# A five-deep weight ring with the rest written over the landed unit, and an earlier gather for the first expert, in a one-core decoder layer

## The chip, the cores and the metric

The kernel runs on one core of one Trainium2 chip. The metric is the device time of one execution in microseconds (us). The core has five engines that run their own instruction streams and meet at semaphores: TensorE (PE in the rows, its weight loads PEld), VectorE (DVE), ScalarE (ACT), GpSimd (POOL) and SyncE (SP, which here only issues DMAs). MB is 10^6 bytes.

## The reference

One layer of a decoder on 256 tokens of width 2048, all in float32:

```
h = RMSNorm(x);  p = h @ W_in          # latent q and kv of MLA, rope key, stick-breaking q, k, v
x = x + concat(RMSNorm(o_MLA), RMSNorm(o_SB)) @ W_out      # 8 heads each, causal
x = x + MemCrossAttn(RMSNorm(x), RMSNorm(mem))             # 4 heads into 256 memory tokens
x = x + HierMoE(RMSNorm(x))            # 4 groups x 8 experts: top-1 group, then top-2 in it
y = RMSNorm(x)                         # an expert: (silu(t @ w_gate) * (t @ w_up)) @ w_down
```

Each of the 32 experts has 4.19 MB in each of w_gate, w_up and w_down: 12.6 MB an expert, 403 MB in all. They are read whatever the routing.

## The kernel before

**The first part, the projections.** A projection is a chunk of 512 columns (chunk KV_LAT has 320), and a chunk is cut into units of two 128-row tiles of the weight: 138 units, numbered in the order of `UNITS`. A unit passes through three rings of `RING` = 4 slots: SP loads it into `w_raw` (line 399), ACT rounds it into `w_hi` (`rounded`, line 1084), DVE writes the rest `w_raw - w_hi` into `w_lo` (`split_w`, line 1452), and PE multiplies hi by hi, hi by lo and lo by hi (lines 546 to 548, and 751 to 753 for one token tile alone). SP loads unit u once unit u-4 is split (semaphore `w_split`); ACT rounds unit u once unit u-4 is used by PE (`w_used`). ACT and DVE run their other work in program order: `rounded(upto)` and `split_w(upto)` stand between the other steps and name the unit up to which the engine goes on before it does the next step. Nearly all of these calls ask for `RING` units more than PE has done at that point.

**What lies between the units.** After the query latent, DVE turns the rotary part of the queries (`rope`, lines 1504 to 1509) at step (Q_PE, 1) of the loop over `LATENT`. The attention runs in a loop of nine steps over 8 heads; PE multiplies two units of the memory projections in each head, and units 90 and 91 of the output projection (W_OUT, 0) and (W_OUT, 1) in the last one. The units of MEM_O are 130 to 137; PE takes 130 to 133 first for token tile 0 and then for token tile 1, and only the second counts as used.

**Transfers ahead.** SP's queue is in order. 16 pieces of 0.5 MB of expert 0 are issued after weight units 102 to 130. After the last weight unit it issues the other half of expert 0's gate and up (`load_first`, 2 x 2.1 MB), then expert 1's gate and up into `gu[1]`, which lies over the weight rings: 1 MB when the memory attention has its values, 2.1 MB when all units are split, 2.1 MB when all but two are used, 3.1 MB at the last. Then expert 2 goes into the buffers of expert 0, in pieces that wait for `first_used` (line 459), which PE counts as expert 0's first k tiles are multiplied.

**Routing and expert 0.** From the router's logits DVE finds the group and the two experts of each token (`max`, `max_index`, `picks`, `sel`), PE ranks the tokens of each expert by multiplying a triangular matrix with `sel` (lines 906 and 907), DVE makes the one-hot matrix `hot_0` of expert 0's tokens (line 1886), PE gathers them (930), ACT copies (1377), PE turns (938), DVE applies the gain (`xe`, 1917), and PE starts expert 0 (953). `keep_running` issues matmuls whose result nobody reads. The expert loop then takes one expert after the other with two weight buffers.

Of the kernel before, what the change touches and what calls it, by code (L numbers as in the profile page):

```python
# [45 lines left out]
RING = 4  # L46
# [68 lines left out]
def layer(nc, x, mem, positions, norm_mix, w_in, norm_q_lat, w_q_b, norm_kv_lat, w_kv_b,  # L115
# [11 lines left out]
    with ctx:  # L127
# [27 lines left out]
        v_mem = place("v_mem", [P, TT, UN])  # L155
        ident = place("ident", [P, P])
# [71 lines left out]
        o_mem = place("o_mem", [P, TT, UN], offset=w_at + 48 * 1024)  # L228
        memo_lo = place("memo_lo", [P, MEM_HEADS, SEQ], F32R, offset=w_at + 52 * 1024)
# [14 lines left out]
        x_slots_0 = place("x_slots_0", [P, UN], offset=sb_mask_at)  # L244
# [104 lines left out]
        def _(sp):  # L349
# [33 lines left out]
            for u, (c, i) in enumerate(UNITS):  # L383
# [6 lines left out]
                if u >= RING:  # L390
                    sp.wait_ge(S("w_split"), u - RING + 1)
# [41 lines left out]
            def load_quarter(b, m, q):  # L433

                w = (w_gate, w_up)[m][0, 1].rearrange("(p k) f -> p (k f)", k=KD)
                k0 = b * KD // 2 + 4 * q
                sp.dma_start(gu[1][:, b, m, 4 * q:4 * q + 4, :].rearrange("p k f -> p (k f)"),
                             w[:, k0 * FE:(k0 + 4) * FE]).then_inc(S(f"gu_loaded1{b}"), 16)
# [12 lines left out]
            load_quarter(1, 0, 0)  # L451
            load_quarter(1, 1, 0)
# [47 lines left out]
        def _(pe):  # L500
# [394 lines left out]
            for t in range(TT):  # L895
# [4 lines left out]
            keep_running(1, 12)  # L900


            pe.wait_ge(S("chosen"), 1)
            sel = rt[:, 528:528 + TT * EXPERTS]
            pe.wait_ge(*chunk_out(CHUNKS - 1))
            pe.matmul(ps[2][:, 0:TT * EXPERTS], before, sel, start=True, stop=False)
            pe.matmul(ps[2][:, EXPERTS:TT * EXPERTS], ones[:, :], sel[:, 0:EXPERTS], start=False,
                      stop=True).then_inc(S("ranked"), 1)
            pe.matmul(ps[3][:, 0:EXPERTS], ones[:, :], sel[:, 0:EXPERTS], start=True, stop=False)
            pe.matmul(ps[3][:, 0:EXPERTS], ones[:, :], sel[:, EXPERTS:TT * EXPERTS], start=False,  # L910
                      stop=True).then_inc(S("counted"), 1)


            def gather(n, first=False):

                if first:
                    pe.wait_ge(S("last_copied"), TT)
                else:
                    pe.wait_ge(S("hot_ready"), n + 1)
                    pe.wait_ge(S("xe_ready"), n)  # L920
                for t in range(TT):
                    if first:
                        pe.wait_ge(S("hot_0_ready"), t + 1)
                    for g in range(NJ):
                        if first:
                            h, rows = hot_0[:, t, :], x_res[:, t, g * UN:(g + 1) * UN]
                        else:
                            h, rows = hot[:, t, :], h_nat[:, t, 4 * g:4 * g + 4, :].rearrange(
                                "p k d -> p (k d)")
                        mm = pe.matmul(ps[4][g * SLOTS:(g + 1) * SLOTS, :], h, rows,  # L930
                                       start=(t == 0), stop=(t == TT - 1))
                mm.then_inc(S("gathered"), 1)

            def gather_turn(n, slots=x_slots):

                pe.wait_ge(S("slots_copied"), n + 1)
                for j in range(NJ):
                    mm = pe.transpose(ps[4][:, j * P:(j + 1) * P], slots[:, j * P:(j + 1) * P],  # L938
                                      ident[:, :])
                mm.then_inc(S("slots_turned"), 1)  # L940

            def gate_up(b, side, loads, first=False):
# [4 lines left out]
                else:  # L947
                    more = 16 + 16 * b
# [114 lines left out]
            expert(0, 0, 1)  # L1063
# [7 lines left out]
        def _(sc):  # L1071
# [95 lines left out]
            rounded(DONE[Q_LAT] + RING)  # L1167
# [31 lines left out]
            for n, (c, i) in enumerate(LATENT):  # L1199
                rounded(POS[(c, i)] + RING)  # L1200
# [28 lines left out]
            for i in range(HEADS + 1):  # L1229
                if i < HEADS:  # L1230
                    rounded(START[MEM_K] + 2 * i + RING)
# [9 lines left out]
                if i == HEADS:  # L1241
                    rounded(START[MEM_K] + 2 * i + RING)
# [30 lines left out]
            rounded(POS[(W_OUT, 1)] + RING)  # L1273
            head_norm(HEADS - 2)
            rounded(POS[(W_OUT, 2)] + RING)
            head_norm(HEADS - 1)
            rounded(POS[(W_OUT + 1, 0)] + RING)
# [8 lines left out]
            for c in range(W_OUT, MEM_Q):  # L1286
                rounded(DONE[c] + RING)
                if c > W_OUT and (c - W_OUT) % 2 == 0:
                    memx_heads((c - W_OUT) // 2 - 1)
            rounded(START[MEM_Q] + 3 + RING)  # L1290
# [49 lines left out]
            for q in range(1, 4):  # L1340
                rounded(DONE[MEM_O + q - 1] + RING)
# [24 lines left out]
            scaled(0)  # L1366
            sc.wait_ge(S("logits_ready"), 1)
# [4 lines left out]
            def slots_copy(n, first=False):  # L1372
                sc.wait_ge(S("gathered"), n + 1)
                if not first:
# [785 lines left out]
```

## Time and profile before

| | |
|---|---|
| median of 3 runs | 1401.48 us (1400.82 to 1402.10) |
| profiled execution, its own time | 1399.43 us |
| its span, first to last instruction | 1397.4 us |
| time around the span | 2.0 us |
| PE busy, share of the span | 1063.6 us, 76% |
| DVE, ACT busy | 535.0 us, 336.2 us |
| mean granted TensorE clock | 0.906 of full |
| bytes moved | 481.71 MB, mean 345 GB/s |

All times in the rows are from the start of the span of that one execution. A released wait is told in brackets: how long the engine was idle before the instruction, and what ended it.

### The profile page before, as it was taken

The numbers are of one execution on the slowest core, as the hardware profiler recorded it, in microseconds if no ns is written. First come the engines' busy times: TensorE is split into PE (matmuls) and PEld (weight loads), VectorE is DVE, ScalarE is ACT, GpSimd is POOL, SyncE is SP. The second block draws the span as 40 slices with busy tenths as digits, with TensorE's granted clock in tenths as the row PEclk, the third lists the DMA queues.
The fourth block names the chain that finished last, engine by engine and source line by source line (L and its number), as shares of the span: only waits on it lengthen the run. The fifth ranks groups of instructions, "written<-read, shape, count | busy, mean of one in ns | idle before, by whom it ended". The sixth has DMA issues, their size and how long they took to land.

```text
span 1397.4 us, 21679 instructions
## 1 busy us (share of the span) xinstructions
PE 1063.6 (76%) x8760; PEld 637.4 (46%) x8760; DVE 535.0 (38%) x1110; ACT 336.2 (24%) x607; POOL 33.5 (2%) x96
## 2 busy tenths in 40 slices
PE   8999999999999987575665667665666656666555
PEld 7888887878888632232322223222222222222222
DVE  5545576566665543222222222222222222223223
ACT  5654456665455401000000000000000000000002
POOL 1000000110001000000000000000000000000001
PEclk9999999999999999888888788888888887889878
DMA  7866653326875899999999999999999999999996
GB/s 239 276 195 181 179 167 109 94 85 234 274 290 187 336 424 427 426 425 425 425 430 426 425 425 426 429 426 426 426 425 426 428 426 426 426 426 428 425 426 288
DMA packets 92468, 481.71 MB, mean 345 GB/s; under 512 B 11590, under 2 KB 21964, under 8 KB 59916
## 3 DMA queue, kind: packets, MB, share of 16 engines
q1 hardware_dynamic: 91932, 478.75, 85.9%
q10 hardware_dynamic: 304, 2.11, 0.4%
q0 software_dynamic: 192, 0.31, 0.1%
q8 instruction: 26, 0.43, 0.1%
q14 instruction: 14, 0.11, 0.0%
HBM read 479.04 MB, written 2.10 MB: 344 GB/s over the span
## 4 chain that ended last, share of the span: by engine, by line
DMA 44%; PE 40%; SPq 6%; ACT 4%; DVE 3%; issue 2%; POOL 0%; ACTq 0%; POOLq 0%; DVEq 0%
DMA gu<-in_w_up 42%; PE ps L546 7%; PE ps L548 7%; PE ps L547 7%; PE ps L953 5%; SPq L413 5%; PE ps L1011 4%; PE ps L930 2%; DMA down<-in_w_down 1%; DVE w_lo L1452 1%; SPq L423 1%; PE ps L513 1%; PE ps L938 1%; PE ps L751 1%; PE ps L753 1%
## 5 line engine op out<-in xcount | busy, mean ns | idle before, releaser
L953 PE MATMUL ps<-gu,xe 128*32 128x256 f32 x4096 | 316.1, 477 | 237.9 <-DMA gu<-in_w_up 237.8
L953 PEld LDWEIGHTS ps<-gu,xe 128*32 128x32 f32 x4096 | 153.2, 136 | 422.4 <-DMA gu<-in_w_up 285.0
L1926 DVE TENSOR_TENSOR x_res<-ps,x_res 128x512 f32<-128x512 f32 x248 | 154.0, 683 | 413.1 <-PE ps L965 413.1
L1452 DVE TENSOR_TENSOR w_lo<-w_raw,w_hi 128x1024 fp32r<-128x1024 f32 (+1 forms) x138 | 164.3, 1200 | 129.9 <-ACT w_hi L1084 127.1
L546 PE MATMUL ps<-w_hi,a_hi 128*128 128x512 f32 (+1 forms) x472 | 185.0, 392 | 0.3 <-DVE w_lo L1452 0.3
L547 PE MATMUL ps<-w_lo,a_hi 128*128 128x512 f32 (+1 forms) x472 | 181.4, 384 | 0.0
L548 PE MATMUL ps<-w_hi,a_lo 128*128 128x512 f32 (+1 forms) x464 | 178.4, 385 | 0.0
L1084 ACT ACTIVATE w_hi<-w_raw 128x1024 fp32r<-128x1024 f32 (+1 forms) x138 | 142.1, 1039 | 130.3 <-PE ps L548 116.5
L1384 ACT ACTIVATE sg<-ps 128x128 f32<-128x128 f32 x31 | 8.6, 278 | 607.9 <-PE ps L953 607.9
L1011 PE MATMUL ps<-down,turned 128*32 128x512 f32 x1024 | 117.2, 595 | 28.6 <-ACT turned L1390 24.4
L546 PEld LDWEIGHTS ps<-w_hi,a_hi 128*128 128x128 f32 x472 | 88.7, 188 | 19.3 <-issue 3.2
L547 PEld LDWEIGHTS ps<-w_lo,a_hi 128*128 128x128 f32 x472 | 88.9, 188 | 16.1
L548 PEld LDWEIGHTS ps<-w_hi,a_lo 128*128 128x128 f32 x464 | 87.2, 188 | 17.4
L965 PE MATMUL ps<-y_sb,turned 32*128 32x512 f32 x496 | 71.7, 647 | 23.5 <-ACT y_sb L1393 23.5
L1011 PEld LDWEIGHTS ps<-down,turned 128*32 128x32 f32 x1024 | 30.6, 109 | 94.2 <-issue 80.1
L1956 DVE TENSOR_TENSOR act<-sg,ps 128x128 f32<-128x128 f32 x31 | 8.9, 287 | 151.7 <-ACT sg L1384 151.7
L930 PE MATMUL ps<-h_nat,hot 128*32 128x512 f32 x496 | 58.9, 592 | 0.0
L1917 DVE TENSOR_TENSOR xe<-ps,g_ffn 128x128 f32<-128x128 f32 x124 | 27.4, 283 | 76.2 <-PE ps L938 76.2
L965 PEld LDWEIGHTS ps<-y_sb,turned 32*128 32x128 f32 x496 | 20.0, 184 | 63.9 <-issue 38.0
L1393 ACT ACTIVATE y_sb<-ps 128x512 f32<-128x512 f32 x31 | 18.5, 597 | 123.6 <-PE ps L1011 123.6
L938 PE MATMUL ps<-ident,x_slots 128*128 128x128 f32 x128 | 21.0, 286 | 22.3 <-ACT x_slots L1377 22.3
L938 PEld LDWEIGHTS ps<-ident,x_slots 128*128 128x128 f32 x128 | 13.4, 141 | 50.4 <-ACT x_slots L1377 50.4
(305 smaller groups left out, 840.5 us busy)
## 6 DMA issues: line engine op xcount, KB each, us to landing
down<-in_w_down SPq DMA_DIRECT2D x124, 1024.0 KB, 23.6
gu<-in_w_gate SPq DMA_DIRECT2D x61, 2048.0 KB, 31.6
gu<-in_w_up SPq DMA_DIRECT2D x60, 2048.0 KB, 36.0
w_raw<-in_w_in SPq DMA_DIRECT2D x56, 512.0 KB, 3.8
w_raw<-in_w_out SPq DMA_DIRECT2D x32, 512.0 KB, 4.8
w_raw<-in_w_mem_kv SPq DMA_DIRECT2D x16, 512.0 KB, 3.8
gu<-in_w_up SPq DMA_DIRECT2D x5, 1024.0 KB, 10.4
down<-in_w_down SPq DMA_DIRECT2D x8, 512.0 KB, 5.6
```

Of the source, the lines that this page charges most:

```text
L413: sp.dma_start(gu[side][:, b, m].rearrange("p k f -> p (k f)"), w[:, b * half:(b + 1) * half]).then_inc(S(f"gu_loaded{side}{b}"), 16)
L546: pe.matmul(acc[t][:, 0:n], xh, wh, start=(k == 0), stop=False)
L547: pe.matmul(acc[t][:, 0:n], xh, wl, start=False, stop=False)
L548: mm = pe.matmul(acc[t][:, 0:n], xl, wh, start=False, stop=(k == kn - 1))
L930: mm = pe.matmul(ps[4][g * SLOTS:(g + 1) * SLOTS, :], h, rows, start=(t == 0), stop=(t == TT - 1))
L938: mm = pe.transpose(ps[4][:, j * P:(j + 1) * P], slots[:, j * P:(j + 1) * P], ident[:, :])
L953: mm = pe.matmul(ps[5][j * SLOTS:(j + 1) * SLOTS, 0:2 * P].rearrange("s (m f) -> s m f", m=2), xe[:, k, :], gu[side][:, b, :, kk, j * P:(j ...
L965: return pe.matmul(ps[g][:, :], turned_6[rows, t, :], y_sb[rows, :], start=True, stop=True)
L1011: mm = pe.matmul(ps[7][g * SLOTS:(g + 1) * SLOTS, :], act_t[:, j * SLOTS:(j + 1) * SLOTS], w[:, jj, g * UN:(g + 1) * UN], start=(j == 0), ...
L1084: sc.activation(w_hi[:, u % RING, :, 0:n], w_raw[:, u % RING, :, 0:n], ACT.Copy).then_inc(S("w_rounded"), 1)
L1452: ve.tensor_tensor(w_lo[:, u % RING, :, 0:n], w_raw[:, u % RING, :, 0:n], w_hi[:, u % RING, :, 0:n], ALU.subtract).then_inc(S("w_split"), 1)
L1926: ins = ve.tensor_tensor(xs, ps[g][:, :], xs, ALU.add)
```

## The change

Three things, all shown below in the core of the diff.

1. The rings have five slots, and there are two of them: `w_lo` lies at the address of `w_raw`, so the rest is written over the landed unit. SP may load unit u only when unit u-5 is used by PE (`w_used`), where it waited for a split before. The calls of `rounded` and `split_w` ask for `LEAD` = 3 units ahead in place of 4. `nat`, `km_t`, `v_mem`, `o_mem` and `memo_lo` move down by 8 KB a partition.
2. Expert 1's gate and up are cut otherwise: 1 MB (k tiles 4 to 8 of the last quarter, in the 8 KB that came free) goes right after `load_first(0)`, 1 MB when the memory attention has its values, 2.1 MB when all but three units are used, 1 MB when all but two, 3.1 MB at the last.
3. Expert 0's tokens are found by two comparisons, group 0's logit against the largest group logit and expert 0's against the second largest of its group, ahead of the rest of the routing. PE ranks this one column, the gather goes in two halves with two copies and two turns, and the ranking of all experts (`rank_all`) comes after the gather on PE. The loads of the loop counts on PE, ACT and DVE move behind expert 0.

```diff
-RING = 4
+RING = 5
+LEAD = 3
...
         w_raw = place("w_raw", [P, RING, UK, UN])
+        w_lo = place("w_lo", [P, RING, UK, UN], F32R, offset=w_at)
         w_hi = place("w_hi", [P, RING, UK, UN], F32R)
-        w_lo = place("w_lo", [P, RING, UK, UN], F32R)
...
+        at[0] = w_at + 64 * 1024
...
                 if u >= RING:
-                    sp.wait_ge(S("w_split"), u - RING + 1)
+                    sp.wait_ge(S("w_used"), u - RING + 1)
...
             sp.wait_ge(S("mem_scored"), 4)
             load_first(0)
+            load_rows(1, 1, 4, 8)
             sp.wait_ge(S("mem_o"), 4)
-            load_quarter(1, 1, 1)
-            sp.wait_ge(S("w_split"), len(UNITS))
-            load_gate_up(1, 1, halves=(0,), sides=(0,))
+            load_rows(1, 1, 0, 4)
+            sp.wait_ge(S("w_used"), len(UNITS) - 3)
+            load_rows(1, 0, 0, 4)
+            load_rows(0, 0, 6, 8)
+            load_rows(0, 1, 0, 2)
             sp.wait_ge(S("w_used"), len(UNITS) - 2)
-            load_quarter(0, 1, 1)
-            load_quarter(1, 0, 1)
+            load_rows(0, 0, 0, 2)
+            load_rows(0, 1, 2, 4)
             sp.wait_ge(S("w_used"), len(UNITS))
-            load_quarter(0, 1, 0)
-            load_quarter(1, 0, 0)
-            load_quarter(1, 1, 0)
+            load_rows(0, 0, 2, 6)
+            load_rows(0, 1, 4, 8)
+            load_rows(1, 0, 4, 8)
...
-            keep_running(1, 12)
+            keep_running(1, 6)
...
+            chosen_0 = rt[:, 320:320 + TT]
+            pe.wait_ge(S("first_chosen"), 1)
+            pe.matmul(ps[2][:, 0:TT], before, chosen_0, start=True, stop=False)
+            pe.matmul(ps[2][:, 1:TT], ones[:, :], chosen_0[:, 0:1], start=False, stop=True).then_inc(
+                S("first_ranked"), 1)
...
+                for half in range(2):
+                    for t in range(TT):
+                        pe.wait_ge(S("hot_0_ready"), t + 1)
+                        for g in range(NJ):
+                            n0 = g * UN + half * 2 * P
+                            mm = pe.matmul(ps[4 + 2 * half][g * SLOTS:(g + 1) * SLOTS, 0:2 * P],
+                                           hot_0[:, t, :], x_res[:, t, n0:n0 + 2 * P],
+                                           start=(t == 0), stop=(t == TT - 1))
+                    mm.then_inc(S("half_gathered" if half == 0 else "gathered"), 1)
...
-            gather(0, first=True)
-            keep_running(1, 3)
-            gather_turn(0, x_slots_0)
-            keep_running(1, 4)
+            gather_first()
+            rank_all()
+            expert(0, 0, 1)
             pe.wait_ge(S("routed"), 1)
             pairs = pe.value_load(n_iter[0:1, 2:3], min_val=EXPERTS // 2 - 1,
                                   max_val=MAX_PASSES * EXPERTS // 2 - 1)
-            expert(0, 0, 1)
...
             for c in range(Q_LAT, Q_PE):
-                rounded(DONE[c] + RING)
+                rounded(DONE[c] + LEAD)
                 if c == Q_LAT:
                     chunk_copy(c, lambda t: c_q[:, t, :], SS_X)
-                    rounded(DONE[Q_LAT] + RING + 2)
+                    rounded(DONE[Q_LAT] + LEAD + 2)
...
                 if i < HEADS:
-                    rounded(START[MEM_K] + 2 * i + RING)
+                    rounded(START[MEM_K] + 2 * i + LEAD)
...
                 if i == HEADS:
-                    rounded(START[MEM_K] + 2 * i + RING)
+                    rounded(START[MEM_K] + 2 * i + LEAD)
...
             for n, (c, i) in enumerate(LATENT):
-                split_w(POS[(c, i)] + RING)
+                split_w(POS[(c, i)] + LEAD)
...
             for t in range(TT):
-                ins = ve.max(gm8[:, t, :], gl8[:, t, :])
+                ve.max(gm8[:, t, :], gl8[:, t, :])
+                ins = ve.max(m8[:, t, :], el[:, t, 0:PER_GROUP])
             link(ins)
+            ve.tensor_tensor(in_0.rearrange("p (t a) -> p t a", a=1), gl[:, :, 0:1], gm8[:, :, 0:1],
+                             ALU.is_ge)
+            link(ve.tensor_tensor(chosen_0.rearrange("p (t a) -> p t a", a=1), el[:, :, 0:1],
+                                  m8[:, :, 1:2], ALU.is_ge))
+            ve.tensor_tensor(chosen_0, chosen_0, in_0, ALU.mult).then_inc(S("first_chosen"), 1)
...
+            ve.wait_ge(S("first_ranked"), 1)
+            link(ve.tensor_copy(rank_0, ps[2][:, 0:TT]))
+            for t in range(TT):
+                ve.tensor_scalar(hot_0[:, t, :], iota32[:, :], rank_0[:, t:t + 1],
+                                 sel_rstd[:, t:t + 1], ALU.is_equal, ALU.mult).then_inc(
+                                     S("hot_0_ready"), 1)
```

## Rows read from the trace of the kernel before

**Rows 1.** The page's chain that ended last, shares of the span by engine.
```profile
DMA 44%; PE 40%; SPq 6%; ACT 4%; DVE 3%; issue 2%; POOL 0%; ACTq 0%; POOLq 0%; DVEq 0%
```

**Rows 2.** Windows: span, busy us of each engine (count), granted clock, DMA share, GB/s.
```profile
0.00:470.00 470.00, 462.86 (x2335) 385.18 (x2335) 278.16 (x421) 258.06 (x458) 26.93 (x89) 1.00 0.62 200
...
436.00:500.00 64.00, 60.55 (x547) 42.62 (x549) 35.10 (x105) 25.67 (x39) 0.91 (x2) 1.00 0.87 337
445.00:465.00 20.00, 20.00 (x123) 16.23 (x122) 12.68 (x21) 9.93 (x20) 0.00 (x0) 1.00 1.02 398
476.00:483.00 7.00, 6.92 (x98) 4.29 (x93) 4.69 (x26) 5.56 (x3) 0.00 (x0) 1.00 0.21 44
486.00:1375.00 889.00, 576.89 (x6187) 238.55 (x6180) 239.33 (x618) 61.09 (x125) 0.00 (x0) 0.86 1.01 426
```

**Rows 3.** Timeline of ACT, last head and after: start us, us, instruction, [idle before].
```profile
309.57 0.82 ACT L1121 ACTIVATE a_hi<-ps,g_t 128x256 fp32r<-128x256 f32 x2
...
313.83 2.00 ACT L1084 ACTIVATE w_hi<-w_raw 128x1024 fp32r<-128x1024 f32 x2
...
329.74 1.06 ACT L1084 ACTIVATE w_hi<-w_raw 128x1024 fp32r<-128x1024 f32 x1 [1.66 <-PE ps L548]
```

**Rows 4.** Timeline of DVE and then of PE, last head.
```profile
314.90 2.36 DVE L1452 TENSOR_TENSOR w_lo<-w_raw,w_hi 128x1024 fp32r<-128x1024 f32 x2 [2.10 <-ACT w_hi L1084]
...
313.23 0.48 PE L546 MATMUL ps<-w_hi,a_hi 128*128 128x512 f32 x1
```

**Rows 5.** Timeline of DVE through the rotary step, and of PE (its next unit but two).
```profile
193.33 0.43 DVE L1504 TENSOR_TENSOR rope_tmp<-nat,rope_cs 128x256 f32<-128x256 f32 x1 [0.28 <-ACT nat L1128]
...
197.93 1.22 DVE L1452 TENSOR_TENSOR w_lo<-w_raw,w_hi 128x1024 fp32r<-128x1024 f32 x1
...
197.35 0.48 PE L546 MATMUL ps<-w_hi,cq_hi 128*128 128x512 f32 x1
```

**Rows 6.** Timeline of ACT after the query latent, and PE's unit 13.
```profile
40.06 1.36 ACT L1084 ACTIVATE w_hi<-w_raw 128x640 fp32r<-128x640 f32 x2
...
42.60 0.19 ACT L1090 ACTIVATION_READ_ACCUMULATOR v_mla<-c_q 128x1 f32 x1
...
43.65 0.31 PE L546 MATMUL ps<-w_hi,a_hi 128*128 128x320 f32 x1
```

**Rows 7.** Weight loads, issue to landing: three from 54 to 60 us, two from 416 to 430.
```profile
DMA to landing us min/median/max: 7.1/8.2/8.4
...
DMA to landing us min/median/max: 3.6/3.6/3.7
```

**Rows 8.** Timeline of ACT and SP, the last units of the memory projections.
```profile
416.13 1.04 ACT L1084 ACTIVATE w_hi<-w_raw 128x1024 fp32r<-128x1024 f32 x1
...
446.40 1.06 ACT L1084 ACTIVATE w_hi<-w_raw 128x1024 fp32r<-128x1024 f32 x1 [4.93 <-PE ps L753]
...
436.22 5.11 SPq L399 DMA_DIRECT2D w_raw<-in_w_mem_o  x3
441.38 0.47 SPq L429 DMA_DIRECT2D gu<-in_w_up  x1
```

**Rows 9.** Timeline of all engines, routing and expert 0's start.
```profile
473.71 0.23 DVE L1864 TENSOR_TENSOR rt<-rt 128x64 f32<-128x64 f32 x1
...
474.73 0.22 DVE L1884 TENSOR_TENSOR rt<-ps,rt 128x64 f32<-128x64 f32 x1 [0.60 <-PE ps L907]
...
475.44 1.92 PE L930 MATMUL ps<-x_res,hot 128*32 128x512 f32 x16 [0.37 <-DVE hot L1886]
...
479.71 7.11 PE L953 MATMUL ps<-gu,xe 128*32 128x256 f32 x128
...
480.84 0.33 SPq L459 DMA_DIRECT2D gu<-in_w_gate  x1
```

**Rows 10.** Windows of a gap of PE in the expert loop and of what follows it.
```profile
557.50:563.70 6.20, 0.00 (x0) 0.00 (x0) 2.48 (x4) 0.00 (x0) 0.00 (x0) 0.70 1.01 428
563.70:567.00 3.30, 3.25 (x35) 1.54 (x39) 0.00 (x0) 0.00 (x0) 0.00 (x0) 0.53 1.04 442
```

More of the change, by code:

```diff
@@ L899, in _ @@
             mm.then_inc(S("logits_summed"), 1)
-            keep_running(1, 12)
[L903 to L909, printed above, removed]
@@ new lines, in rank_all @@
+            def rank_all():
+                pe.wait_ge(S("chosen"), 1)
+                sel = rt[:, 528:528 + TT * EXPERTS]
+                pe.matmul(ps[2][:, 0:TT * EXPERTS], before, sel, start=True, stop=False)
+                pe.matmul(ps[2][:, EXPERTS:TT * EXPERTS], ones[:, :], sel[:, 0:EXPERTS], start=False,
+                          stop=True).then_inc(S("ranked"), 1)
+                pe.matmul(ps[3][:, 0:EXPERTS], ones[:, :], sel[:, 0:EXPERTS], start=True, stop=False)
+                pe.matmul(ps[3][:, 0:EXPERTS], ones[:, :], sel[:, EXPERTS:TT * EXPERTS], start=False,
+                          stop=True).then_inc(S("counted"), 1)
@@ L921, in gather @@
+            def gather(n):
+                pe.wait_ge(S("hot_ready"), n + 1)
+                pe.wait_ge(S("xe_ready"), n)
                 for t in range(TT):
-                    if first:
-                        pe.wait_ge(S("hot_0_ready"), t + 1)
                     for g in range(NJ):
[L925 to L930, printed above, removed]
+                        mm = pe.matmul(ps[4][g * SLOTS:(g + 1) * SLOTS, :], hot[:, t, :],
+                                       h_nat[:, t, 4 * g:4 * g + 4, :].rearrange("p k d -> p (k d)"),
@@ L1272, in _ @@
             out_head(5)
-            rounded(POS[(W_OUT, 1)] + RING)
+            rounded(POS[(W_OUT, 1)] + LEAD)
             head_norm(HEADS - 2)
-            rounded(POS[(W_OUT, 2)] + RING)
+            rounded(POS[(W_OUT, 2)] + LEAD)
             head_norm(HEADS - 1)
-            rounded(POS[(W_OUT + 1, 0)] + RING)
+            rounded(POS[(W_OUT + 1, 0)] + LEAD)
             out_head(6)
@@ L1286, in _ @@
             for c in range(W_OUT, MEM_Q):
-                rounded(DONE[c] + RING)
+                rounded(DONE[c] + LEAD)
                 if c > W_OUT and (c - W_OUT) % 2 == 0:
                     memx_heads((c - W_OUT) // 2 - 1)
-            rounded(START[MEM_Q] + 3 + RING)
+            rounded(START[MEM_Q] + 3 + LEAD)
             memx_heads(3)
@@ L1340, in _ @@
             for q in range(1, 4):
-                rounded(DONE[MEM_O + q - 1] + RING)
+                rounded(DONE[MEM_O + q - 1] + LEAD + 1)
                 sc.wait_ge(*chunk_out(MEM_O + q - 1))
@@ L1366, in _ @@
             scaled(0)
+            for half, (made, copied) in enumerate((("half_gathered", "half_copied"),
+                                                   ("gathered", "slots_copied"))):
+                sc.wait_ge(S(made), 1)
+                sc.activation(x_slots_0[:, half * 2 * P:(half + 1) * 2 * P], ps[4 + 2 * half][:, 0:2 * P],
+                              ACT.Copy).then_inc(S(copied), 1)
             sc.wait_ge(S("logits_ready"), 1)
@@ L1393, in expert @@
                 sc.activation(y_sb[:, :], ps[7][:, :], ACT.Copy).then_inc(S("y_copied"), 1)
-            slots_copy(0, first=True)
             scaled(1)
+            sc.wait_ge(S("hot_ready"), 1)
+            expert(0)
             sc.wait_ge(S("routed"), 1)
@@ L1624, in _ @@
                     out_rest(5)
-                    split_w(POS[(W_OUT, 1)] + RING)
+                    split_w(POS[(W_OUT, 1)] + LEAD)
                 if i >= 1:
@@ L1876, in gates @@
                 link(ve.tensor_tensor(gate_w[:, 1, :], gate_w[:, 0, :], r2, ALU.mult))
-            ve.wait_ge(S("chosen"), 1)
-            link(ve.tensor_tensor(sel_rstd, sel[:, :, 0:1].rearrange("p t a -> p (t a)"),
-                                  rstd[:, SS_X2:SS_X2 + TT], ALU.mult))
+            by_j = xe[:, :, :].rearrange("p (g j) s -> p j g s", g=NJ)
+            gains = g_t[:, 70:86].rearrange("p (g j) -> p j g", g=NJ)
+            for j in range(NJ):
+                ve.wait_ge(S("half_turned" if j < 2 else "slots_turned"), 1)
+                turned = ps[7 - 7 * (j // 2)][:, j % 2 * P:(j % 2 + 1) * P]
+                ins = ve.tensor_tensor(by_j[:, j], turned.rearrange("p (g s) -> p g s", g=NJ),
+                                       bc(gains[:, j].rearrange("p (g a) -> p g a", a=1), NJ, SLOTS),
+                                       ALU.mult)
+            ins.then_inc(S("xe_ready"), 1)
             ve.wait_ge(S("ranked"), 1)
@@ L1884, in _ @@
             link(ve.tensor_tensor(base_row, rank, bc(r0, TT, EXPERTS), ALU.add))
-            for t in range(TT):
-                ve.tensor_scalar(hot_0[:, t, :], iota32[:, :], base_row[:, t, 0:1],
-                                 sel_rstd[:, t:t + 1], ALU.is_equal, ALU.mult).then_inc(
-                                     S("hot_0_ready"), 1)
             link(ve.tensor_scalar(row, rank, -(SLOTS - 1) / 2.0, 1.0 / SLOTS, ALU.add, ALU.mult))
```

85 lines of the change are left out of this document (43 added, 42 removed).

## The prediction

> **What bounds the kernel now.** I read the chain that ended last, then windows, then timelines around each line that the diff touches. The chain is made of DMA (44%) and PE (40%) [rows 1]. The windows say where each holds: until 470 us PE is busy 462.86 of 470 us at full clock while DMA runs at 62% [rows 2], so that part is as long as PE's own work. From 486 us to 1375 us DMA runs at 426 GB/s, its share 1.01 [rows 2], so that part is bytes over 426 GB/s. Between them lies a hole: 44 GB/s from 476 to 483 us [rows 2]. It ends when PE has used expert 0's first k tiles and SP may send expert 2 (issue at 480.84, expert 0 started at 479.71) [rows 9]. The time is therefore the first part, plus the hole, plus the bytes left. A us that PE loses before 470 us is a us of the kernel; a us won in the routing counts only while the hole is there.
>
> **The ring, where the lead of 3 uncovers PE.** The arithmetic itself costs nothing new: each unit is still one rounding (1.0 us) and one subtraction (1.2 us, [rows 4, 5]) beside 2.72 us of PE (1.06 + 1.66, ACT's pitch where it only follows PE [rows 3]), and writing over an operand changes no shape; I take 0, bounded at 0.1 us a unit, which the same slack would cover. The loads of ring slots are freer for ACT (unit u waits for u-5, no longer u-4), so ACT now passes each call of `rounded` without waiting for PE. But each call goes one unit less far, so that one unit falls behind the next block of other work. I looked at each such block for the unit that is postponed, and set the end of its split against PE's need.
>
> - Unit 91, (W_OUT, 1). Before, it was rounded at the top of the last head but one step; now the call there ends at unit 90, and 91 is rounded after ACT's head work, at the place where 92 stood: ACT works on from 309.57 us (two activations of a_hi, the copy of v_mem, four head norms, the probabilities' copy, the exponential) and reaches the pair at 313.83 us [rows 3]. DVE subtracts the first unit of that pair from 314.90 on [rows 4], so it is split at 314.90 + 1.2 = 316.1. PE wants unit 91 at 313.23 [rows 4]. Nothing can be pulled ahead on PE's in-order stream. Stall: 316.1 - 313.23 = 2.9 us; both chains hang from the head's exponential just ahead of 309.57, so a shift of all leaves it. Bounds 2.5 and 3.2.
> - Unit 68. In step (Q_PE, 1) DVE runs the rotary block from 193.33 us and then subtracts at 197.93 [rows 5]. That subtraction was unit 69's; now it is unit 68's, which PE wants at 197.35 [rows 5]. Stall: 197.93 + 1.2 + 0.05 - 197.35 = 1.85 us. Bounds 1.6 and 2.1.
> - Units 12 and 13. ACT rounded both at 40.06, before the squares of the query latent that end at 42.8 [rows 6]; now 13 comes behind them: rounding 42.8 to 43.5, subtraction (0.83 us for 320 columns) to 44.3, less 0.2 that one rounding fewer gives back: 44.1. PE wants it at 43.65 [rows 6]. Stall 0.4 us. Bounds 0 and 1, as unit 11's load now waits for PE too.
> - The other calls are covered: in heads 1 to 7 the postponed unit is the first of its pair, split as the head's step begins, and PE asks for it only after another unit (2.72 us) and the head's scores; elsewhere a unit has 3 x 2.72 us of PE against at most 5 us of other work plus 2.2 us of rounding and subtraction.
>
> **The ring, the loads.** A load now has from the use of u-5 to the use of u, 4 x 2.72 = 10.9 us, of which rounding and subtraction take 2.3: it must land within 8.5 us. Three loads beside the 2.1 MB of mem took 7.1 to 8.4 us [rows 7]: 0.1 us of stall taken, 0 to 1 as bounds. The Trainium skill, page "DMA: Bandwidth & Descriptors", section "Queues, rings and completion order", says that an engine goes round robin between the queue rows at packet granularity; by that the weight loads keep waiting on mem whatever is queued ahead, and the sum would sit at the upper bound, 0.9 us more. The rows agree that loads are slow there; they don't show the share. In MEM_Q unit 129 is loaded at 412.1 instead of ahead; it was rounded at 416.13 [rows 8], now behind unit 128 and a load that lands about 417.5: rounded by 418.6, split by 419.9 to 420.4, PE's need 419.84: 0.3 us, bounds 0 and 0.7.
>
> PE's part: 2.9 + 1.85 + 0.4 + 0.1 + 0.3 = 5.6 us (bounds 4.1 and 8.0).
>
> **The transfers.** What moves is more than the 1 MB. Units 135 to 137 were issued from 436.22 on, and expert 0's 4.2 MB stood right behind them at 441.38 [rows 8]. In MEM_O only token tile 1 counts as used, so now 135, 136 and 137 wait for the uses at 446.4 (ACT's own wait for that count ended there [rows 8]), 447.8 and 449.1 (one token tile of a unit is 1.36 us of PE), and SP's in-order queue holds `load_first`, the early 1 MB and the rest behind them until 449.5. Those queued units are still in time: a quiet load lands in 3.6 us [rows 7], so 135 is there at 450.5, and PE, which has all of unit 134 (2.72) and the router's turns ahead of it, wants it near 454.9. But DMA loses its time from 438 to 448. Count bytes: from 436 to 500 us 337 GB/s x 64 us = 21.6 MB moved [rows 2]. Now they start to flow at 446.4 + 2.2 = 448.6 (a quiet load's 3.6 us [rows 7] less 1.3 for its 0.52 MB at the 398 GB/s below). The 5.8 MB of 2 KB rows go at 398 GB/s (the window in which such pieces ran [rows 2]): 14.5 us. The other 15.8 MB at 426 [rows 2]: 37.1 us. Sum: 448.6 + 51.6 = 500.2 against 500: +0.2 us, bounds -0.8 and +1.5 (all at 426, or a rate of 385 for the first part). So the hole is gone, filled by transfers that ran in PE's part before; the early 1 MB wins nothing, since it only trades its place in a queue that is now full.
>
> **The routing.** After the logits, DVE has four MAX8 in place of two (+0.24), then three small operations (0.5) instead of the way to `sel` at 473.71 [rows 9]: the column is chosen at 472.25. PE's ranking and DVE's read took 1.02 us for 64 columns (473.71 to 474.73 [rows 9]); for 2 columns 0.8, and a copy 0.2. hot_0 is ready from 473.5, 1.7 us sooner. The gather has the same columns (1.92 us for 16 records [rows 9]); its halves let the first copy (0.4) and turn run beside it: xe ready at 477.05. `rank_all`, 1.1 us, now stands between on PE: expert 0 starts at 477.65, against 479.71 [rows 9]: -2.05 us, bounds -1.2 and -2.7. SP's restart would come at 478.8 (1.1 behind, as 480.84 was) and data at 481.0. The backlog lasts to 482.8 by the count above. So of the 2.05 us nothing is seen in the end; it buys 1.8 us of cover. Were the hole there, all would count. The loop counts are loaded behind expert 0 now, between it and expert 1 on PE, ACT and DVE, with expert 1's projections and down behind them; the rows don't show that load alone, and I bound it by 0 and 2 us, twice the 1.02 us of ranking and read above; what sets the end there is DMA with over 4 MB queued, so I take 0.
>
> **The sum.** Against the profiled execution: span 1397.4 + 5.6 + 0.2 = 1403.2, its own time 1399.43 + 5.8 = 1405.2. That execution lies 2.05 us under the median, so the median goes to 1401.48 + 5.8 = 1407.3, +0.41%. Within 0.2% (2.8 us) is about what a measurement of this kernel can't tell from no change.
>
> **Rivals.**
> - *The stalls are half of it (1403.7).* ACT's and DVE's freer waits let them run ahead enough that units 68 and 91 lose 1.6 us less each and unit 13 nothing (5.8 - 3.2 - 0.4 = 2.2). For: where ACT only follows PE it idles 1.66 us a unit [rows 3], and the wait behind that idle time is relaxed by one unit. Against: in both places the time goes to other work of ACT and DVE, with no PE wait in it but the head's own [rows 3, 5]. Chance 0.12.
> - *The routing gain counts, and the change is faster (1399.4 to 1398.5).* It decides at one point: whether SP sends expert 0's half near 441 or near 449 us, with no stall on PE before. Then the hole of 7 us stays and shrinks by 2.05 to 3 us. Against: the order of SP's code. Chance 0.12, half of it beyond 0.2%.
> - *The stall of 2.9 us costs the clock (1411).* In the expert loop PE idled 6.2 us, in which the granted clock fell (0.70), and the 3.3 us after it ran at 0.53, nearly all at the lower level of 1.2 GHz [rows 10]. Half of such a spell, 1.65 us, is lost; with the loads at their upper bounds (+0.9 and +0.4) and unit 13 at its own (+0.6) that gives 1411. Against: 2.9 us is half that gap, and PE is busy on both sides. Chance 0.06. The Trainium skill, page "TensorE: Matmul & The Clock Gate", section "Why this matters for your kernels", warns of idle gaps between bursts of matmuls as what drops the clock; its rule speaks for this rival, and the rows on 6.2 us agree with it, while none has a single gap of 2.9.
>
> **How the numbers follow.** My own case has 0.70, with 1404.8 to 1411.0 as its range (bounds of PE's part 4.1 and 8.0, of the transfers -0.8 and +1.5). The range over all is 1401.8 to 1411.5. Slower 0.70 + 0.06 = 0.76; same 0.12 + 0.06 = 0.18; faster 0.06.
>
> **What would show it.** Right: PE idle 2.9 us before line 546 with DVE's w_lo as releaser near 313, 1.85 near 197, PE busy still 463 before expert 0 but the start of expert 0 at about 483.2; SP's first `load_first` near 455; DMA at 400 GB/s or more from 456 on without a hole. Wrong: a hole of over 2 us ahead of expert 0, or PE's gaps in the first part under 3 us in sum.

## The result, and the profile after

The changed kernel takes 1410.27 us (median of four runs, 1409.93 to 1410.64) against 1401.50 us (1400.82 to 1402.10): ratio 1.0063, 95% interval 1.0050 to 1.0076. It is 8.8 us slower. Measured twice more beside other runs of before, it was slower by a ratio of 1.0081 (1.0068 to 1.0094) and 1.0074 (1.0061 to 1.0088). The three ratios come to 8.8, 11.4 and 10.4 us. Predicted were +5.8 us, 1407.3, with 1401.8 to 1411.5 as the range: sign and mechanism held, the size fell 3.0 to 5.6 us short. Two single executions, one of before at 2008.74 us and one of lead4_half at 1511.41 us, lie far outside the rest and are in no ratio.

| | before | after |
|---|---|---|
| profiled execution, its own time | 1399.43 us | 1410.28 us |
| its span | 1397.4 us | 1408.5 us |
| mean granted TensorE clock | 0.906 | 0.901 |
| first matmul of expert 0 | 479.71 us | 483.66 us |

The page's chain that ended last, of after, as [rows 1]:

```profile
DMA 44%; PE 36%; SPq 6%; ACT 5%; DVE 3%; issue 2%; POOL 0%; ACTq 0%; POOLq 0%; DVEq 0%
```

PE's share fell by 4 points of the span: in the first part the chain now leaves PE at the units that it waits for, and runs through their load, rounding and subtraction. The windows of after, with the columns of [rows 2]: span, busy us of PE, its weight loads, DVE, ACT and POOL, granted clock, DMA share, GB/s.

```profile
0.00:470.00 470.00, 456.65 (x2283) 379.89 (x2283) 275.73 (x417) 256.32 (x454) 26.45 (x87) 1.00 0.59 187
...
445.00:455.00 10.00, 10.00 (x50) 8.34 (x49) 4.74 (x7) 1.55 (x2) 0.00 (x0) 1.00 0.10 29
455.00:470.00 15.00, 15.00 (x102) 12.14 (x100) 11.17 (x19) 8.33 (x18) 0.00 (x0) 1.00 0.94 345
470.00:500.00 30.00, 26.85 (x307) 16.08 (x307) 15.27 (x78) 13.44 (x17) 0.91 (x2) 1.00 1.02 416
...
486.00:1375.00 889.00, 577.80 (x6189) 238.03 (x6177) 239.86 (x631) 62.47 (x126) 0.00 (x0) 0.85 1.01 426
```

PE is busy 6.21 us less before 470 us than in [rows 2]: so much was lost in the first part. The hole ahead of expert 0 (44 GB/s in [rows 2]) is gone, and another has opened at 445 us, ten microseconds at 29 GB/s. The steady part is unchanged at 426 GB/s.

The timeline of after where PE waits for units 22, 68 and 91, the last with what ACT and DVE did, and then SP, the routing and the start of expert 0:

```profile
66.89 0.47 PE L551 MATMUL ps<-w_hi,a_hi 128*128 128x512 f32 x1 [1.52 <-DVE w_lo L1476]
...
200.99 0.47 PE L551 MATMUL ps<-w_hi,cq_hi 128*128 128x512 f32 x1 [1.70 <-DVE w_lo L1476]
...
317.50 1.99 ACT L1105 ACTIVATE w_hi<-w_raw 128x1024 fp32r<-128x1024 f32 x2
318.58 2.36 DVE L1476 TENSOR_TENSOR w_lo<-w_raw,w_hi 128x1024 fp32r<-128x1024 f32 x2 [2.10 <-ACT w_hi L1105]
319.95 0.47 PE L551 MATMUL ps<-w_hi,a_hi 128*128 128x512 f32 x1 [2.81 <-DVE w_lo L1476]
...
455.93 0.47 SPq L431 DMA_DIRECT2D gu<-in_w_up  x1
...
477.35 0.42 DVE L1862 SCALAR_TENSOR_TENSOR rt<-ps,rstd,b_r 128x36 f32<-128x36 f32 x2 [1.54 <-POOL rstd L2115]
...
479.60 0.51 DVE L1884 TENSOR_SCALAR hot<-iota,rt 128x32 f32<-128x32 f32 x2
480.05 1.93 PE L922 MATMUL ps<-x_res,hot 128*32 128x256 f32 x32 [0.75 <-DVE hot L1884]
483.66 7.11 PE L976 MATMUL ps<-gu,xe 128*32 128x256 f32 x128
484.79 0.33 SPq L464 DMA_DIRECT2D gu<-in_w_gate  x1
```

Each of the first three PE rows is the first matmul of a unit that waited for its subtraction. To see what a wait costs the rest, I compare the starts of the same unit in both kernels. Unit 68 starts at 200.99 against 197.35 [rows 5], 3.64 late; unit 91 at 319.95 against 313.23 [rows 4], 6.72 late. The table does so for every profiled execution: the loss of each place is the lateness behind it less that ahead of it, and the last column is the whole lateness behind the start of unit 135. "Start" is the lateness at unit 2, from the clock of the very first matmuls; negative is earlier.

| lateness against before, us | start | unit 13 | unit 22 | unit 68 | unit 91 | low clock behind it | unit 135 | whole lateness |
|---|---|---|---|---|---|---|---|---|
| after (first profile) | -0.6 | 0.5 | 1.7 | 1.9 | 3.0 | 0 | 0 | 6.5 |
| after_again | -0.6 | 0.5 | 0.7 | 1.9 | 3.0 | 1.6 | 0 | 7.0 |
| after_third | -0.5 | 0.6 | 3.0 | 1.9 | 3.0 | 0 (1.7 behind unit 22) | 0 | 10.1 |
| ring_only | -0.3 | 0.5 | 1.9 | 1.9 | 3.0 | 1.6 | 0 | 8.5 |
| mem4 | -0.4 | 0.6 | 0 | 1.9 | 3.0 | 1.6 | 0 | 6.6 |
| first_early | 0.0 | 0.6 | 1.7 | 1.9 | 3.0 | 1.6 | 2.4 | 11.0 |
| filler | -0.6 | 0.7 | 0.5 | 1.9 | 3.0 | 0 | 0 | 5.4 |
| before_lead3 | -0.3 | 0.4 | 0 | 1.9 | 2.9 | 1.6 | 0 | 6.4 |
| lead4 | 1.7 | 0.1 | 0 | 0 | 0 | 0 | 0.9 | 3.0 |
| lead4_half | -0.4 | 0.2 | 1.4 | 0 | 0 | 0 | 0.9 | 2.3 |
| lead4_first | -0.5 | 0.1 | 0 | 0 | 0 | 0 | 7.7 (1.6 of it low clock) | 7.5 |
| before_late | -0.6 | 0 | 0 | 0 | 0 | 0 | 0.8 | 0.2 |
| routing_only | -0.5 | 0 | 0 | 0 | 0 | 0 | 0 | -0.5 |

The labels are those of the experiments below. That nearly all start 0.3 to 0.6 us earlier says that the profiled execution of before had a slower start than most. Later still, near the turns that PE does at 460 us in before, another 0.3 to 0.8 us are lost in after_again, after_third, ring_only, first_early and before_late, and at most 0.2 us in the others. after_third lost 0.5 us more between units 13 and 22.

### The profile page after: what moved, and what is told of

Its sections match the earlier page's. It is cut to its first block, busy times and chain, and to the rows that moved or that the text cites. A ratio compares the mean times of both kernels' runs of the same rounds, so it can differ in the third digit from the quotient of the medians.

```text
span 1408.5 us, 21676 instructions
## 1 busy us (share of the span) xinstructions
PE 1065.6 (76%) x8754; PEld 635.2 (45%) x8754; DVE 535.6 (38%) x1116; ACT 336.2 (24%) x608; POOL 33.5 (2%) x96
## 4 chain that ended last, share of the span: by engine, by line
DMA 44%; PE 36%; SPq 6%; ACT 5%; DVE 3%; issue 2%; POOL 0%; ACTq 0%; POOLq 0%; DVEq 0%
DMA gu<-in_w_up 42%; PE ps L551 6%; PE ps L553 6%; PE ps L552 6%; SPq L415 5%; PE ps L976 5%; PE ps L1034 4%; PE ps L952 2%; DMA down<-in_w_down 2%; DVE w_lo L1476 1%; SPq L425 1%; DMA w_raw<-in_w_in 1%; ACT w_hi L1105 1%; PE ps L961 1%; PE ps L756 1%
```

## The experiments

**One part of the change alone.** routing_only is the kernel before with the third part of the change and nothing else; ring_only is the changed kernel with the old routing.

> The kernel before with only the third part of the change (expert 0's tokens by two comparisons, gather in halves, rank_all behind it); rings and transfers untouched. Theory: the hole of 7 us ahead of expert 0 stays and its end moves with the routing, so the 2.5 us between the logits and expert 0 that the changed kernel shows (6.31 against 8.82 us) all count: 1401.5 - 2.5 = 1399.0 us (1398.6 to 1399.6), DMA low from 476 to about 480.5 us. Rival (the loop counts loaded behind expert 0, or a ranking that now stands between, take it back): 1401.5 us.

Measured: 1399.16 us, ratio 0.9984 (0.9975 to 0.9993). The gain counts as long as the hole is there. Timeline and windows of routing_only:

```profile
473.03 1.93 PE L917 MATMUL ps<-x_res,hot 128*32 128x256 f32 x32 [0.75 <-DVE hot L1879]
...
476.65 7.11 PE L971 MATMUL ps<-gu,xe 128*32 128x256 f32 x128
477.78 0.33 SPq L459 DMA_DIRECT2D gu<-in_w_gate  x1
```

```profile
476.00:480.50 4.50, 4.50 (x79) 2.97 (x82) 3.95 (x22) 3.29 (x1) 0.00 (x0) 1.00 0.44 129
```

SP restarts at 477.78 instead of 480.84 [rows 9]: 3.06 us, of which 0.55 is the start of the execution and 2.5 the routing. This is the fastest kernel of the study, 2.2 us (1.0 to 3.5) under before.

> The changed kernel with the old routing: rings, lead and transfers as changed. Theory: the changed kernel's queue is full until some 490 us and expert 0 would free the first buffers near 487, so the routing gain is hidden: the same 1410.3 us (1409.9 to 1411.0), no hole of more than 1 us ahead of expert 0's successor. Rival (the end of the routing sets the end there too): 1410.3 + 2.5 = 1412.8 us.

Measured: 1412.06 us, ratio 1.0084 (1.0071 to 1.0098). The time lies nearer the rival's 1412.8 than the theory's 1410.3, but it can't decide: the changed kernel itself came out at 1.0063, 1.0081 and 1.0074. The profile speaks for the theory. It has no hole (414 GB/s from 480 to 490 us), and counted in bytes moved by 560 us its stream is 2.1 us later than its PE was at unit 135 (10.7 against 8.5 us), as in after (8.6 against 6.5), with the old routing and with the new. So the routing gain is hidden by the full queue, as predicted. The higher time stays unexplained: the low clock behind unit 91 is in the profiled execution too, and that was the fastest of the five (1409.45 us).

**The lead.** lead4 sets `LEAD = 4` in the changed kernel; before_lead3 is the kernel before with three rings of four and the calls one unit shorter.

```
-LEAD = 3
+LEAD = 4
...
-                rounded(DONE[MEM_O + q - 1] + LEAD + 1)
+                rounded(DONE[MEM_O + q - 1] + LEAD)
```

> The changed kernel with LEAD = 4 in place of 3 (the two rings of five stay, the rounding of MEM_O's units goes as far as it did). Theory: the stalls of PE for units 13, 68 and 91 (0.38, 2.03 and 3.08 us by the start of the waiting matmul against the kernel before) come from the postponed unit alone and go; the wait near 65 us (1.75) and the late transfers stay: 1410.3 - 5.3 = 1405.0 us (1404.5 to 1405.8). Rival (they come from loads that wait for PE's use and are not landed in time): 1410 us, with the same gaps.

> The kernel before, three rings of four, with every call of the rounding and of the subtraction going one unit less far (LEAD = 3), nothing else. Theory: the stalls at units 68 and 91 (2.03 + 3.08, less some 0.2) and at unit 13 (0.4) appear without any change of ring or load, the hole ahead of expert 0 stays and every us of PE counts: 1401.5 + 5.3 = 1406.8 us (1406.0 to 1407.5). Rival (the deeper ring and the loads behind PE's use make them): 1401.5 us.

Measured: lead4 1403.97 us, ratio 1.0026 (1.0016 to 1.0036); before_lead3 1407.29 us, ratio 1.0043 (1.0030 to 1.0057). Both theories hold: the stalls at units 13, 68 and 91 go with the lead and come with it (table). Of before_lead3:

```profile
199.33 0.47 PE L547 MATMUL ps<-w_hi,cq_hi 128*128 128x512 f32 x1 [1.70 <-DVE w_lo L1453]
...
318.31 0.47 PE L547 MATMUL ps<-w_hi,a_hi 128*128 128x512 f32 x1 [2.70 <-DVE w_lo L1453]
```

```profile
318.30:322.00 3.70, 3.69 (x11) 2.90 (x12) 2.92 (x4) 3.61 (x11) 0.00 (x0) 0.63 0.59 206
```

The last row was new to me: behind the stall the granted clock is 0.63 for 3.7 us, most of it at 1.2 GHz, and 1.6 us more are lost. With 5.2 us of stalls (units 13, 68 and 91) that makes 6.8 us in this execution; the ratio says 6.0 us (4.2 to 8.0). lead4 came out 1.0 us under its expectation: the wait at unit 22, which I had let stand (1.75 us), went too in that execution, and unit 135 came 0.9 us late.

**The wait at unit 22.** mem4 asks for mem in four parts.

```
-                    sc.dma_start(mem_sb[:, :, :], mem[0].rearrange("(t p) d -> p t d", p=P)).then_inc(
-                        S("mem_loaded"), 16)
...
+                if KV_LAT <= c < KV_LAT + 4:
+                    cols = slice((c - KV_LAT) * UN, (c - KV_LAT + 1) * UN)
+                    sc.dma_start(mem_sb[:, :, cols], mem[0, :, cols].rearrange(
+                        "(t p) d -> p t d", p=P)).then_inc(S("mem_loaded"), 16)
```

> The changed kernel with the 2.1 MB of mem asked for in four parts of 0.5 MB, one after each of four chunks, in place of one request. Theory: PE's wait of 1.75 us near 65 us comes from that request beside the weight loads that have one unit less of lead, and goes; all else stays: 1410.3 - 1.7 = 1408.6 us (1408.0 to 1409.3), the unit's loads landing in under 5 us there. Rival (loads that wait for PE's use are late without any other transfer): 1410.3 us and the same gap.

Measured: 1408.96 us, ratio 1.0060 (1.0047 to 1.0072), beside 1.0081 (1.0068 to 1.0094) of the changed kernel in the same comparison. The two intervals touch, so it is the profile that settles this: the wait at unit 22 is gone, with the low clock behind unit 91 in both profiles. Time from issue to landing of the weight loads from 52 to 60 us, in after, after_third and mem4:

```profile
DMA to landing us min/median/max: 4.6/7.6/9.9
```

```profile
DMA to landing us min/median/max: 4.6/10.6/11.7
```

```profile
DMA to landing us min/median/max: 4.5/4.8/5.8
```

With the one request a load takes up to 9.9 or 11.7 us, with the parts 5.8 at most. The wait is not one size: 0.5 to 3.0 us over the six executions with the one request and LEAD = 3, and even with LEAD = 4 it was 1.4 us once and nothing in two. The four kernels with rings of four (before, routing_only, before_lead3, before_late) never show it; there a load may be issued as soon as a split is done, and in before_lead3 landings of 8.1 to 8.4 us in the same stretch held nothing up. mem4 makes the request smaller and also spreads it over four chunks, so it ties the wait to that request, not to its size alone.

**The transfers.** before_late adds one wait to the kernel before:

```
+                if u >= len(UNITS) - 3:
+                    sp.wait_ge(S("w_used"), u - RING)
```

> The kernel before with one added wait: the loads of weight units 135, 136 and 137 wait for PE's use of units 130, 131 and 132, as they do in the changed kernel, so that expert 0's first half and expert 1 stand in SP's queue behind them until about 449.5 us. Nothing on PE changes. Theory: this alone is the transfer term; the ramp of the 2 KB rows from rest costs more than the 398 GB/s of a later window, and the stream ends 2.0 to 2.2 us later: 1401.3 + 2.1 = 1403.4 us (1402.8 to 1404.0), the hole from 476 to 483 us gone. Rival (the prediction's count): +0.2, 1401.5 us.

Measured: 1401.75 us, ratio 1.0004 (0.9995 to 1.0013). My theory by now was wrong and the prediction's count (+0.2) was right. Windows of before_late: DMA stands from 440 us, and then has no hole at all.

```profile
440.00:448.00 8.00, 8.00 (x38) 6.65 (x37) 3.52 (x5) 1.66 (x2) 0.00 (x0) 1.00 0.11 32
476.00:486.00 10.00, 9.91 (x142) 6.08 (x146) 6.02 (x32) 5.57 (x3) 0.00 (x0) 1.00 1.01 417
```

What had misled me is the profiled execution of before itself. These are the first 10 us from SP's restart at expert 0, in before, routing_only, before_lead3 and lead4_half, each with a hole ahead of it:

```profile
480.84:490.84 10.00, 8.70 (x139) 4.64 (x131) 2.80 (x13) 3.52 (x5) 0.00 (x0) 1.00 0.92 339
```

```profile
477.78:487.78 10.00, 8.70 (x139) 4.64 (x131) 5.23 (x28) 4.15 (x5) 0.00 (x0) 1.00 0.83 283
```

```profile
487.18:497.18 10.00, 8.70 (x138) 4.64 (x130) 2.80 (x13) 3.52 (x5) 0.00 (x0) 1.00 0.82 279
```

```profile
480.60:490.60 10.00, 8.70 (x138) 4.64 (x130) 5.22 (x28) 4.23 (x5) 0.00 (x0) 1.00 0.86 289
```

In the profile of before the stream picked up at 339 GB/s, in these three at 279 to 289, and in the two more that have such a hole (lead4_first and first_early) at 308 and 332. Their mean is 298: 0.41 MB less in 10 us, 1.0 us at 426 GB/s. So the 2.1 us by which after's stream is later than its PE are some 1.1 us against a usual restart. By this, an estimate from the mean, the profiled execution of before owes about 1.0 of its 2.05 us under the median to its own restart (0.2 to 1.4 against the single rates).

first_early, lead4_first and lead4_half move expert 0's first half ahead of the last three weight units:

```
                 if u in EARLY_AT:
                     early_piece(EARLY_AT.index(u))
+                if u == FIRST_AFTER:
+                    sp.wait_ge(S("w_used"), START[MEM_O])
+                    load_first(1)
+                    sp.wait_ge(S("mem_scored"), 4)
+                    load_first(0)
+                    load_rows(1, 1, 4, 8)
```

`FIRST_AFTER` is 134. lead4_half has only the first two of the moved lines there; its other three stay behind the last unit. Both kernels named lead4 have `LEAD = 4` as above.

> The changed kernel with one thing moved in the order of SP's queue: expert 0's first half (2 x 2.1 MB) and the 1 MB of expert 1 are issued behind weight unit 134 in place of behind 137, so ahead of the three units that wait for PE's use. Theory: they fill the 10 us in which DMA stood (445 to 455 us at 2 and 57 GB/s), the three units land in time, all of expert 1 has been sent before expert 0 frees a buffer, and a hole of 3 to 5 us comes back ahead of that point (484.8 us in the changed kernel, 480.84 before): 1401.2 + 4.0 = 1405.2 us (1404.5 to 1406.5). Rival (units 135 to 137 now land behind 5 MB and PE waits for them in MEM_O for 3 us or more): 1408 to 1411 us.

> The same move together with LEAD = 4. Theory: PE's first part is then within 0.5 us of the kernel before, the hole is back, and the routing gain of 2.5 us counts as it did with the old rings (there 1.8 us in the time): 1401.0 - 1.5 = 1399.5 us (1398.8 to 1400.5). Rival (the loads behind PE's use go on costing 1.5 us or more): 1401 us or above.

> The changed kernel with LEAD = 4 and only the first 2.1 MB of expert 0 moved behind weight unit 134; the other 2.1 MB and expert 1 stay behind unit 137. Theory: 2.1 MB issued at 429 us is over by 437, ahead of unit 135 at 446, so no weight unit is late; the stream gains up to 5 us on the run with LEAD = 4 alone (1404.0) and is then bounded by the release of expert 0's buffers, at 478.7 us: 1399.8 us (1399 to 1401). Rival (weight units still land late behind it, 5.9 us of PE in the run that moved all): 1402.5 us or more.

Measured: first_early 1410.04 us, ratio 1.0068 (1.0056 to 1.0080); lead4_first 1407.34 us, ratio 1.0051 (1.0036 to 1.0066), slower than lead4; lead4_half 1400.63 us, ratio 0.9997 (0.9987 to 1.0006). With 5.2 MB ahead the rival came true, in lead4_first in full, in first_early by its time alone (PE stood 2.1 us, not 3). Of lead4_first, PE's wait in the timeline, the 3.5 us behind it, the three units' loads from issue to landing, and the window ahead of SP's restart at 485.81:

```profile
459.69 1.97 PE L856 MATMUL ps<-ident,x_res 128*128 128x128 f32 x8 [5.88 <-DVE x_res L1791]
```

```profile
459.69:463.20 3.51, 3.51 (x13) 3.14 (x14) 3.51 (x6) 1.42 (x4) 0.00 (x0) 0.51 0.71 291
```

```profile
DMA to landing us min/median/max: 8.8/8.9/9.0
```

```profile
482.00:486.00 4.00, 3.88 (x56) 2.56 (x52) 3.37 (x18) 3.52 (x6) 0.00 (x0) 1.00 0.35 143
```

Units 135 to 137, issued from 446.14 on, landed 8.8 to 9.0 us later, PE stood 5.9 us and then ran at a granted clock of 0.51 for 3.5 us, and the hole ahead of expert 0 was back besides. With 2.1 MB ahead nothing but the 0.9 us at unit 135 is seen, and the time is 3.3 us better than lead4's by the medians. The hole at 445 us is not worth that by itself: before_late has it and loses nothing. With it gone the stream waits for expert 0 again (the hole ahead of SP's restart at 480.60), so that the routing gain of 2.5 us counts; these runs don't split the 3.3 us between the two. lead4_half and before can't be told apart.

**The clock.** filler puts matmuls that nobody reads into the stall ahead of unit 91; after_again and after_third are the changed kernel once more.

```
                     out_turn(5)
+                    pe.wait_ge(S("probs_copied"), HEADS)
+                    keep_running(4, 9)
                     project_out(W_OUT, 1)
```

> The changed kernel once more, for a second profiled execution beside the same runs of before as the others. Theory: ratio as measured, 8.8 to 10.5 us over the kernel before; the stall of 3 us at unit 91 is followed by matmuls at the lower clock in some executions (1.6 us more, as in two of three profiled executions that have this stall) and not in others, so single times spread between about 1409.5 and 1412.5 us. Rival (the clock fell for another reason): no such spread, and no second level in the single times.

> The changed kernel with nine matmuls whose result nobody reads (128 columns each, 2.5 us together) between PE's work of the last head and unit 91, in the stall. Theory: PE is then idle for under 0.8 us there and its granted clock stays at 2.4 GHz from 320 to 324 us, where it was at 1.2 GHz in three of five profiled executions with this stall: 1.6 us less than the changed kernel beside it in those executions, the mean 0.8 to 1.6 us less. Rival (the fall has another cause): clock and time as the changed kernel's.

> The changed kernel beside the run with the filler. Both theories: 1410.3 to 1412 us, 9 to 10.5 us over the kernel before; it is here for the comparison alone.

Measured: after_again 1411.83 us (1411.25 to 1413.34), after_third 1411.45 us (1409.77 to 1414.04), filler 1409.02 us (1408.75 to 1410.71), ratio 1.0063 (1.0049 to 1.0076). The windows are of after and after_again behind the stall at unit 91; of after_third in the wait at unit 22 and behind it; of filler behind unit 91.

```profile
319.95:323.60 3.65, 3.65 (x20) 3.14 (x21) 2.91 (x4) 3.56 (x11) 0.00 (x0) 1.00 0.02 4
```

```profile
318.90:321.90 3.00, 2.98 (x8) 2.40 (x9) 2.93 (x4) 2.91 (x11) 0.00 (x0) 0.55 0.00 1
```

```profile
65.70:68.90 3.20, 0.41 (x3) 0.05 (x1) 1.23 (x1) 1.93 (x2) 0.00 (x0) 1.00 0.83 251
69.70:73.30 3.60, 3.60 (x11) 2.78 (x10) 3.41 (x4) 2.80 (x3) 0.00 (x0) 0.53 0.06 17
```

```profile
318.90:325.00 6.10, 6.07 (x33) 5.24 (x34) 4.59 (x9) 4.17 (x14) 0.00 (x0) 1.00 0.27 87
```

The same stall of 2.8 us is followed by the full clock in one execution and by 0.55 in the next. Over all profiled executions of this study the 2.7 to 2.8 us at unit 91 were followed by some 3.5 us at the low level in five of seven (the expectation's three of five was a miscount); none of the eight waits of 1.7 us at unit 68 was, and filler, where PE was idle 0.43 us, was not. One profile of filler doesn't prove that the filler did it; its time is 2.4 us under the changed kernel's beside it by the medians and 1.5 by the ratios, whose intervals overlap, and waits at unit 22 of other sizes (0.5 against 3.0 us in the profiles) may be a part of that. So the clock's fall behind the stall is measured, and what decides whether it comes is not shown.

## Why the prediction was right, and where it was short

- **What bounds the kernel.** Right. A us lost on PE in the first part was a us of the kernel; the routing gain counted with the hole (routing_only) and, by the bytes moved in ring_only and after, not without it.
- **Unit 91, 2.9 us.** Right: 2.9 to 3.0 in all eight executions with `LEAD = 3`. ACT's pair began at 317.50 and DVE's subtraction at 318.58, each 3.7 us later than in [rows 3, 4], with PE 3.67 us late by then. before_lead3 and lead4 show that the lead alone makes it.
- **Unit 68, 1.85 us.** Right: 1.9. Unit 13, 0.4: 0.4 to 0.7. Unit 129, 0.3: nothing was lost there.
- **The mem request, 0.1 us, bounds 0 and 1.** The step that failed most. It cost 1.7 us in the first profile, 0.5 to 3.0 in all. I took landings of 7.1 to 8.4 us from [rows 7] against 8.5 us of room and let the mean decide, where one load of three is enough; and those landings were those of a kernel that issued its loads sooner. Now they took up to 9.9 and 11.7 us. The Trainium skill, page "DMA: Bandwidth & Descriptors", section "Queues, rings and completion order", has each DMA engine go round robin between the queue rows at packet granularity. The prediction took that as a sign for its upper bound; the direction was right, and the size (1.7 us) lay above that bound too. No run here shows how the engines shared their time.
- **The transfers, +0.2 us, bounds -0.8 and +1.5.** Right in order and timing: `load_first` was issued at 455.93, the predicted 449.5 plus the 6.46 us that PE was late; the hole is gone; the change of order alone gave +0.6 us (-0.7 to +1.8) in before_late. Against the profiled execution of before it seemed 2.1; some 1.0 of that was its quick restart. The rate was wrong where the stream begins: I counted 398 GB/s from its first byte and named 400 from 456 us on as a sign of being right. With both loads of `load_first` (4.2 MB) issued by 457.1 us it still ran at 308 GB/s until 462, and at 394 only behind that. Against 398 these five us alone are short by 0.45 MB, 1.1 us, about what is left of the 2.1:

```profile
457.00:462.00 5.00, 5.00 (x31) 4.34 (x30) 4.53 (x7) 3.86 (x8) 0.00 (x0) 1.00 0.89 308
```

- **Units 135 to 137 in time.** Right in after. In before_late, lead4 and lead4_half unit 135 started 0.8 to 0.9 us late, behind turns that waited 0.6 to 0.7 us for DVE's `x_res`: the addition stood behind the subtraction of a unit whose load had come later.
- **The routing, 2.05 us and hidden.** Right in kind; 2.5 us in size: 6.31 us from the first operation on the logits (477.35) to expert 0 (483.66), against 8.82 us from the same operation (470.89) to [rows 9].
- **The sum.** PE's part was 5.6 us in the prediction and 7.1 in the first profile (6.5, and 0.6 for the start). The mem request is the difference (1.6; the others cancel). With 1.1 us of transfers that makes 8.2 of the 8.8 us, in an execution without the low clock. The clock comes on top in other executions: I gave "the stall costs the clock" 0.06 and priced it at 1.65 us. Price right (1.6), chance wrong: it came in five of seven. It was never an alternative to my case but a term of it, to be taken at its price times its chance. The Trainium skill, page "TensorE: Matmul & The Clock Gate", section "Why this matters for your kernels", warns of idle gaps between bursts of matmuls as what drops the clock; the windows above agree, for most executions and not for all.
- **The span.** It grew by 11.1 us, the median by 8.8. The two profiled executions also differ in the last half expert, 64 matmuls each, first before, then after, with their windows:

```profile
1370.60 3.66 PE L953 MATMUL ps<-gu,xe 128*32 128x256 f32 x64 [2.76 <-DMA gu<-in_w_up]
```

```profile
1370.60:1374.30 3.70, 3.70 (x65) 2.09 (x66) 0.00 (x0) 0.00 (x0) 0.00 (x0) 1.00 1.01 421
```

```profile
1379.94 5.35 PE L976 MATMUL ps<-gu,xe 128*32 128x256 f32 x64 [3.55 <-DMA gu<-in_w_up]
```

```profile
1379.90:1385.30 5.40, 5.36 (x65) 2.73 (x65) 0.00 (x0) 0.00 (x0) 0.00 (x0) 0.68 1.02 425
```

It ran at full clock in before and at 0.68 in after, which takes 1.7 us. This tail came at either clock in seven of the fourteen profiled executions. It was quick in all four with the old routing (before, before_lead3, before_late, ring_only) and in three of the ten with the new (first_early, lead4, lead4_half), and slow in the other seven, all three of the changed kernel among them. So I can't say that the 1.7 us are no part of the change. A quick restart (1.0), a quick tail (1.7) and a slower start (0.6) would make the 2.05 us by which the profiled execution of before lies under its median, but before_late had the quick tail too and lay at its own median (1401.64 against 1401.75 us).

What stays open: how far the unit 22 wait and the low clock share the spread of 1409.8 to 1414.0 us of the changed kernel's single times, since only the profiled ones show either; why the stream picks up at 339 GB/s in one execution and 280 in others; and whether the slow tail comes with the new routing or by chance. If it comes with the routing, up to 1.7 us of the loss are its, and the sum above has too much elsewhere.

## What to carry to other kernels

A lookahead written into the program of an in-order engine is worth what stands behind its last unit: shorten it by one, and look at each block of other work for the unit that now falls behind it; deeper rings don't give it back. A gain in front of a full queue buys nothing, and the same gain in front of an idle queue buys nearly its full size, so the third part of the change alone beats both kernels. A single profiled execution can lie 2 to 3 us under its kernel's median (2.05 in before, 2.6 in ring_only): compare its own time with the median before taking a difference of spans apart.

## What the runs showed of the hardware

- Of eight waits of 2.7 to 2.8 us without a matmul six were followed by some 3.5 us mostly at 1.2 GHz, which cost 1.6 us (1.7 in after_third), and two by none. The 5.88 us of lead4_first were followed by it and cost no more, 1.6 us. The eight waits of 1.7 us at unit 68 and the 2.13 us of first_early were not.
- A queue that starts again from rest ahead of expert 0, gated by the use of buffers, moved 279 to 339 GB/s in its first 10 us against 413 in the same stretch of before_late, whose queue had not run dry there. Where it started again near 454 us in after, with more issued than it moved, it gave 308 GB/s from 457 to 462 us. The row is that of before_late:

```profile
481.40:491.40 10.00, 8.70 (x138) 4.64 (x131) 2.80 (x13) 3.52 (x5) 0.00 (x0) 1.00 1.02 413
```

- A weight load of 0.5 MB landed after 3.6 us in quiet [rows 7], after up to 11.7 us beside one request of 2.1 MB, and after 9 us behind 5.2 MB issued before it on the same queue.
